# Row factors of a norm: from products with diagonal matrices to a store and a broadcast load

## The reference

```
def rms_norm(x, g):
    xf = x.astype(jnp.float32)
    y = xf * lax.rsqrt(jnp.mean(xf * xf, axis=-1, keepdims=True) + RMS_EPS)
    return (y * g.astype(jnp.float32)).astype(x.dtype)

def mixer_sublayer(x, norm_g, w_in, sinks, rel_bias, pool_w, pool_scale, w_out):
    h = rms_norm(x, norm_g)
    z = h @ w_in
    qa, ka, va, qr, kr, vr, gr, up = jnp.split(z, SPLIT_POINTS, axis=-1)
    ...
    return x + y @ w_out
```

## Time and profile before

| | |
|---|---|
| median of 3 runs | 2024.3 us (2023.88 to 2024.69) |
| profiled execution, its own time | 2023.26 us |
| its span | 2021.5 us, 26909 instructions |
| TensorE (PE) busy | 2009.1 us, 99% |
| VectorE (DVE) busy | 1416.7 us, 70% |
| ScalarE (ACT) busy | 890.3 us, 44% |
| GpSimd (POOL) busy | 190.0 us, 9% |
| granted TensorE clock, mean | 0.999 of full speed |

### The profile page before, as it was taken

How to read it: one execution, slowest core, us unless ns; L and a number is a source line. 1 busy time by engine, 2 the same in 40 slices (tenths; PEclk the granted TensorE clock), 3 DMA queues, 4 the chain that set the end, 5 groups by cost and what they waited for, 6 DMA issues and landing times.

```text
span 2021.5 us, 26909 instructions
## 1 busy us (share of the span) xinstructions
PE 2009.1 (99%) x9980; PEld 1693.3 (84%) x9980; DVE 1416.7 (70%) x2043; ACT 890.3 (44%) x1500; POOL 190.0 (9%) x279
## 2 busy tenths in 40 slices
PE   9999999999999999999999999999999999999998
PEld 8988898889889888888888888888888888888886
DVE  5685578558746977777778677677666668667667
ACT  5433543534354426545456544445333334433333
POOL 1042113203220330000000000000000000000001
PEclk9999999999999999999999999999999999999999
DMA  7133412522352233676856566787956578756572
GB/s 282 53 105 127 151 63 73 190 88 75 104 187 79 87 120 103 150 180 162 178 152 151 135 152 177 175 190 203 391 202 271 196 302 319 288 204 259 200 290 84
DMA packets 101950, 348.64 MB, mean 172 GB/s; under 512 B 10267, under 2 KB 12220, under 8 KB 84412
## 3 DMA queue, kind: packets, MB, share of 16 engines
q1 hardware_dynamic: 99372, 338.27, 52.4%
q10 hardware_dynamic: 2448, 8.65, 1.2%
HBM read 270.21 MB, written 76.68 MB: 172 GB/s over the span
## 4 chain that ended last, share of the span: by engine, by line
PE 97%; DVE 1%; ACT 1%; issue 0%; DMA 0%; POOL 0%; POOLq 0%; ACTq 0%; SPq 0%; DVEq 0%
PE bank L2140 30%; PE bank L2142 29%; PE bank L2141 29%; PE bank L2237 1%; PE bank L2265 1%; PE bank L2313 1%; PE bank L2294 1%; PE bank L2316 1%; PE bank L2280 1%; PE bank L2356 1%; PE bank L2321 1%; PE bank L2251 1%; DVE hT_lo L1443 1%; PE bank L2130 0%; PE bank L2341 0%
## 5 line engine op out<-in xcount | busy, mean ns | idle before, releaser
L2140 PE MATMUL bank<-h_hi,w_lo 128*128 128x512 f32 x912 | 355.9, 390 | 1.1 <-ACT tA L1137 0.9
L2142 PE MATMUL bank<-h_hi,w_hi 128*128 128x512 f32 x912 | 354.9, 389 | 0.0
L2141 PE MATMUL bank<-h_lo,w_hi 128*128 128x512 f32 x912 | 354.9, 389 | 0.0
L2140 PE MATMUL bank<-d_hi,u_lo 128*128 128x512 f32 x896 | 348.5, 389 | 0.0
L2141 PE MATMUL bank<-d_lo,u_hi 128*128 128x512 f32 x896 | 348.5, 389 | 0.0
L2142 PE MATMUL bank<-d_hi,u_hi 128*128 128x512 f32 x896 | 348.5, 389 | 0.0
L1904 DVE TENSOR_TENSOR u_lo<-u_raw,u_hi 128x1024 fp32r<-128x1024 f32 x112 | 137.0, 1223 | 180.1 <-ACT u_hi L1286 180.1
L1286 ACT ACTIVATE u_hi<-u_raw 128x1024 fp32r<-128x1024 f32 x112 | 118.6, 1059 | 327.9 <-PE bank L2142 315.7
L2140 PE MATMUL bank<-ring_hi,hT_lo 128*128 128x384 f32 (+1 forms) x672 | 241.3, 359 | 0.0
L2142 PE MATMUL bank<-ring_hi,hT_hi 128*128 128x384 f32 (+1 forms) x672 | 234.1, 348 | 0.0
L2141 PE MATMUL bank<-ring_lo,hT_hi 128*128 128x384 f32 (+1 forms) x672 | 233.8, 348 | 0.0
(11 more groups left out here) (220 smaller groups left out, 3111.5 us busy)
## 6 DMA issues: line engine op xcount, KB each, us to landing
u_raw<-u_dram SPq DMA_DIRECT2D x56, 1024.0 KB, 4.8
d_raw<-in_wdn SPq DMA_DIRECT2D x56, 1024.0 KB, 6.9
stage<-in_wmix SPq DMA_DIRECT2D x108, 512.0 KB, 4.4
u_dram<-ur SPq DMA_DIRECT2D x32, 1280.0 KB, 9.7
wraw<-in_wup SPq DMA_DIRECT2D x128, 256.0 KB, 3.9
e_raw<-in_wdn SPq DMA_DIRECT2D x24, 1024.0 KB, 8.9
xq<-in_x SPq DMA_DIRECT2D x16, 512.0 KB, 3.6
x_dram<-xq ACTq DMA_DIRECT2D x16, 512.0 KB, 3.1
```

Source lines behind the costliest of these rows:

```text
L2140: pe.matmul(dst, al, bh, start=(first and k == 0), stop=False, skip_group_check=chain)
L2141: pe.matmul(dst, ah, bl, start=False, stop=False, skip_group_check=chain)
L2142: last = pe.matmul(dst, ah, bh, start=False, stop=(final and k == n - 1), skip_group_check=chain)
```

## The change

The diagonals, the products with ones and the copy go. In their place ScalarE stores the four columns of `rstd` to DRAM as 512 consecutive numbers (`store_factors`), and loads them back as one row, repeated for all 128 partitions, straight into `rb` (`load_factors`). Both transfers are issued from ScalarE's queue: the store behind tile 2's evacuation, the load behind the split of unit 5, where ScalarE first waits for the store. GpSimd's first factor of a quarter waits for the store of the quarter before. The waits that the products carried for T1 move to the second transposes of the attention.

```
+    factors_dram = nc.dram_tensor("row_factors_dram", (NQ, NB, P), F32).ap()
...
-        diag_done = Events(sem("diag_done"), 4)
-        rbmm_done = Events(sem("rbmm_done"), 1)
-        rb_done = Events(sem("rb_done"), 1)
+        rf_stored = Events(sem("rf_stored"), 1, 16)
+        rb_done = Events(sem("rb_done"), 1, 16)
...
+                if b == 0:
+                    pool.wait_ge(rf_stored.sem, rf_stored.before(q, 0))
                 pool.tensor_tensor(rstd[:, b:b + 1], var[:, b:b + 1], mhalf[:, 0:1], ALU.pow).then_inc(rstd_done.sem, 1)
-
-            def diagonal(q, b):
-
-                pool.wait_ge(rstd_done.sem, rstd_done.now(q, b))
-                if b == 0:
-                    pool.wait_ge(qk_done.sem, qk_done.before(q, 3))
-                    pool.wait_ge(rbmm_done.sem, rbmm_done.before(q, 0))
-                pool.tensor_tensor(dg[:, b, :], ident[:, :], rstd[:, b:b + 1].to_broadcast([P, P]), ALU.mult).then_inc(diag_done.sem, 1)
...
-            def rb_copy(q):
-
-                act.wait_ge(rbmm_done.sem, rbmm_done.now(q, 0))
+            def store_factors(q):
+
+                act.wait_ge(rstd_done.sem, rstd_done.now(q, NB - 1))
+                act.dma_start(factors_dram[q].rearrange("b p -> p b"), rstd[:, 0:NB], allow_slow_non_contiguous=True).then_inc(rf_stored.sem, 16)
+
+            def load_factors(q):
+
+                act.wait_ge(rf_stored.sem, rf_stored.now(q, 0))
                 ev, k = evac_of(T_UP1)
                 act.wait_ge(ev.sem, ev.before(q, k))
-                act.activation(rb[:, :], T1[:, :], ACT.Copy).then_inc(rb_done.sem, 1)
+                row = factors_dram[q:q + 1].rearrange("a b p -> a (b p)")
+                act.dma_start(rb[:, :], row.to_broadcast([P, QT])).then_inc(rb_done.sem, 16)
...
                 evac_T(q, 2)
+                store_factors(q)
                 split_hi(q, 5)
+                load_factors(q)
                 split_hi(q, 6)
-                rb_copy(q)
                 split_hi(q, 7)
...
-            def row_factors(q):
-
-                pe.wait_ge(qkT_evac.sem, qkT_evac.before(q, 7))
-                pe.wait_ge(yPlo_done.sem, yPlo_done.before(q, 1))
-                pe.wait_ge(s_brow, NQH)
-                pe.wait_ge(s_init, 2)
-                pe.wait_ge(diag_done.sem, diag_done.now(q, NB - 1))
-                for b in range(NB):
-                    last = pe.matmul(T1[:, b * P:(b + 1) * P], ones[:, :], dg[:, b, :], start=True, stop=True)
-                last.then_inc(rbmm_done.sem, 1)
...
                 elif i == 1:
-                    pe.wait_ge(rb_done.sem, rb_done.now(q, 0))
+                    pe.wait_ge(qkT_evac.sem, qkT_evac.before(q, 7))
+                    pe.wait_ge(yPlo_done.sem, yPlo_done.before(q, 1))
...
                 for t in range(4):
                     proj_T(q, t)
-                row_factors(q)
                 proj_T(q, 4)
```

More of the change, by code:

```diff
@@ L161, in build @@
         rt = work("rt", 179200, [P, 2, 6 * P])
-        dg = work("dg", 179200, [P, NB, P])
         thb = work("thb", 185344, [P, 2, 3 * P])
@@ L792, in _ @@
         def _(pool):
-            for e in (diag_done, rstd_done, rstd2_done, var2_done, var_done, rotB_done, kz_done,
+            for e in (rstd_done, rstd2_done, var2_done, var_done, rotB_done, kz_done,
                       rg_done, v6_done, r6_done, s6_done, win_done):
@@ L835, in rot_b @@
                     pool.wait_ge(tab_full.sem, tab_full.now(q, 0))
-                    pool.wait_ge(rbmm_done.sem, rbmm_done.now(q, 0))
                     evacuated(pool, q, T_GROUP + 7)
@@ L894, in mixer_pool @@
                     inv_rms(q, b)
-                    diagonal(q, b)
                 rot_b(q, 0)
@@ L945, in _ @@
         def _(act):
-            for e in (sq_done, rb_done, xhi_done, whi_done, z_evac, v_evac, exp_done, yAhi_done, qkT_evac,
+            for e in (sq_done, rf_stored, rb_done, xhi_done, whi_done, z_evac, v_evac, exp_done, yAhi_done, qkT_evac,
                       osb_done, sqr_done, th_done, yRhi_done, yPhi_done, sq2_done, *x2_stored):
@@ L2124, in _ @@
         def _(pe):
-            for e in (rbmm_done, tile_done, vtr_done, s_done, ptr_done, o_done, qktr_done, rs_done, ro_done, ru_done,
+            for e in (tile_done, vtr_done, s_done, ptr_done, o_done, qktr_done, rs_done, ro_done, ru_done,
                       ytr_done, mix_done):
```

## The result

The kernel takes 2049.07 us after the change (median of 5 runs, 2045.74 to 2050.25), against 2024.3 us before (median of 5 runs, 2023.44 to 2024.69): 24.8 us or 1.2% slower, ratio 1.012 with a 95% interval of 1.0109 to 1.013. The prediction had been 2021.3 us, range 2020.2 to 2026.0.

What follows compares the result with a forecast made beforehand. TensorE's own work was taken as the bound, busy 2009.1 of 2021.5 us. Removed products -3.6 and quarter 1's weight delay +0.6 took the profiled 2023.26 to 2020.3, or 2021.3 us at the median; range 2020.2 to 2026.0.

Steps and rivals of the forecast that it cites:

- the size of the store: Time for ScalarE's store of 512 4-byte pieces to land in DRAM: 3.3 us, bounded by 1.7 and 6.8.
- The price of a small packet, 13 ns: Cost per packet below 512 bytes, from DMA traffic at 22 to 26 us; 32 per engine cost 0.4 us, taken four times.
- the load was put at 3.1 us: Broadcast load of 256 KB into rb: bounded by 2.2 and 5.7 us, taken as 3.1.
- The round trip is too long: Rival, 0.14: store and load exceed 9.3 us before the scores, costing their excess each quarter; upper bounds give +9.2 us, 2033.5.
- the removed products: TensorE's four products between tiles 3 and 4 go, saving 0.89 us a quarter, 3.6 us in four.
- The budget of 9.3 us: Quarter 2's time for store, wait and load, from 218.7 to rb's deadline of 228.0; same distances in quarters 3 and 4.
- ScalarE's blocked splits: Splits 6 to 8 queue behind the store wait; unit 6's low half still ends at 224.7 in quarter 2, ahead of rb.
- Quarter 1 as the narrow place: kT there follows unit 6's low half, leaving little slack before the scores; a weight delay loses 0.6 us.
- the weights of unit 6 behind the load: In quarter 1 the load's 256 KB delay the weight transfer by 0.65 us, of which 0.6 is lost.
- The 0.06 us of slack: Quarter 1: kT ends at 40.35 and the scores, moved up by 0.89, want to start at 40.41.
- these delays cost nothing: Units 6 to 8, delayed by ScalarE's wait, are first used after tile 5, some 5 us behind the scores.
- The fixed cost of about 2 us: Trainium skill's DMA cost, mostly the write's receipt; by it alone the store would take 2 us, the saving unchanged.

Runs made afterwards that it cites:

- store_only: Kernel before the change, products and copy kept, with the 4-byte store added behind tile 2's evacuation and its data used by no engine: 2030.58 us, ratio 1.0035.
- a16_order: 16-byte-piece kernel with full output, plus quarter 1's bias-row loads moved behind unit 6's weights on the sync queue: 2020.26 us, ratio 0.9981.
- load_only: Changed kernel without the store; the broadcast load waits for no store and reads 512 numbers of an input: 2020.83 us, ratio 0.9982.
- pad64: Changed kernel with the 512 4-byte pieces stored 64 bytes apart and rb loaded from an input: 2021.73 us.
- a16: Changed kernel with a partition's four factors stored as one 16-byte piece, the row read by VectorE with a stride, full output: 2021.64 us, ratio 0.999.
- a16_early: 16-byte-piece kernel with the store moved ahead of tile 2's evacuation and the load ahead of unit 5's split: 2023.46 us, ratio 0.9994.

## Why the prediction was wrong

**The step that failed** is the size of the store: "1.7 + 1.6 = 3.3 us", with 6.8 us as its upper bound. It measured 8.8 us (up to 11.8). The price of a small packet, 13 ns, came from packets that were mostly reads, and the upper bound scaled with the number of pieces. Neither knows of the thing that counts, how near to each other the pieces are written. For pieces 64 bytes apart the store took 3.1 us, near the estimate; the four-fold price of a packet in it was a guess that no run tests. A second step was mis-sized too: the load was put at 3.1 us (2.5 to 4.5) and took 5.0 as a median and 9.3 in quarter 1.

**The rival named for this side was right in kind and too cheap.** "The round trip is too long" had 0.14. Its price at the upper bounds was 3.2 us of excess in each quarter and +9.2 us. The round trips were 8.8 + 9.3 = 18.1 us in quarter 1, 11.8 + 3.3 = 15.1 in quarter 2, 8.2 + 5.1 = 13.3 in quarter 3 and 8.8 + 4.9 = 13.7 in quarter 4. Two costs stood at nothing in its price: the clock, 10.3 us in all, by which the wait of 5.2 us in quarter 2 costs 7.3, and the hold on the sync queue, 6.5 us by itself in store_only (with the slow matmuls behind its wait).

**Right:** the removed products, 0.89 us a quarter: a16_order, with no wait left at the scores, gains 3.8 us. The budget of 9.3 us with kT as the gate: in quarters 2 to 4 the round trips pass it by 5.8, 4.0 and 4.4 us and TensorE waits 5.2, 3.3 and 3.8. The 0.6 to 0.7 us between them fit the moment at which the store left: the sum put it at the end of tile 2's evacuation, and it left at its start, 0.60 us earlier. ScalarE's blocked splits: in quarter 2 the low half of unit 6 ended at 242.17, ahead of rb at 242.7, as the order of the queues said. Quarter 1 as the narrow place.

**Right in mechanism, wrong in size:** the weights of unit 6 behind the load, 0.6 us predicted, 1.8 us measured in load_only. The 0.06 us of slack ahead of it leave out the hand-over of 0.10 us that the same prediction counts in quarter 2; with it there was none.

**Wrong:** "these delays cost nothing" of the weights. It was argued from ScalarE's wait alone; in quarter 1 unit 6 came at 45.24 in place of 37.44 because the store kept the DMA engines, and there it, not rb, was the last to arrive (kT at 47.48 follows directly behind its low half of 46.33).

**The rule of the Trainium skill.** Its page DMA: Bandwidth & Descriptors, Rules for kernel authors, has one descriptor for each element of a strided last dimension; the trace agrees, with 528 packets on the scalar queue while the store of 512 pieces goes on. Its Specifications name a read-modify-write below 512 bytes. Every store here has pieces below 512 bytes, and those of pad64 and a16 land in about 3 us, so being under that size alone doesn't give the 8.8 us; whether it is such a read-modify-write that neighbours wait for, no run shows. The fixed cost of about 2 us that the prediction takes from the anatomy of a DMA on the same page of the Trainium skill stands there in a section on transfers issued by GpSimd; those here leave from ScalarE, and their stores in pieces of 16 bytes landed in 2.4 to 2.8 us in a16 and in 1.4 to 5.2 in a16_early.

## What to carry to other kernels

When a store goes to DRAM in pieces of a few bytes, look at how near the pieces lie to each other more than at their number: four factors of a partition written as one 16-byte piece cost 2.6 us, the same numbers in 4-byte neighbours 8.8 us. Price a new transfer on three accounts: its own chain, what it does to the transfers beside it (here the weights of unit 6, with no slack), and, if TensorE is going to wait for it, the slow matmuls after the wait. A transfer kept out of the critical chain can still cost: the dead store lost 6.5 us.

## What the runs showed of the hardware

- The more 4-byte writes lie close together in DRAM, the later the store lands: 0.43 us for each further one in 64 bytes with 128 pieces, 0.38 with 512; that they are written one after the other within a small region, of 32 to 512 bytes, is the reading that fits, and was not seen directly.
- While they go on, the DMA engines count as busy and move little (0.96 busy, 46 GB/s in store_only), also for the other queue: the 128 KB loads of the bias rows landed in 8.0 us in place of 2.2.
- After idling 8.0 us TensorE had 0.50 of its clock from its start at 48.3 to 52 us and 1.00 again from 54; in quarter 3 a wait of 3.3 us was followed by a loss of 2.8 us, and in a16_early one of 2.7 us by a loss of 1.6.
- A DMA that stands behind an activation in ScalarE's list left when the activation began (227.56), not when it ended (228.16).
